# Differential attention: copies of turned probabilities ahead of exponentials, gate and half chunks ending ahead of scores

## The chip, the cores and the metric

One core of a Trainium2 chip runs the whole program. The metric is device time in microseconds (us), the median of several runs. TensorE does the matrix products, VectorE (DVE in the profile) and ScalarE (ACT) the elementwise work, GpSimd (POOL) prepares the weights, SyncE (SP) issues the weight transfers. Each engine works through its own queue in order and waits on semaphores for the others.

## The reference

One step of a streaming encoder with two layers over 544 tokens (512 of a prompt, 32 of a sample), width 1024. The change lies in the second ("odd") layer, whose mixer is, cut down:

```
z = h @ w_in                                    # h: normed input
cq, ck, cv, cg, cr, dq, dk, dv = split(z)       # cg: gate of the linear attention
og = rms_norm(gla(cq, ck, cv, cr)) * silu(cg)   # 4 chunks of 128 features
p  = softmax(mask(q @ k.T / 8))                 # differential attention: 4 heads, 2 maps each
a  = p[:, :, 0] - lam * p[:, :, 1]
od = rms_norm(a @ v) * (1 - lambda_init)
y  = concat([og, od]) @ w_out
x  = x + y
```

The mask is causal by chunks of 64, so the query block b of 128 tokens reads (b + 1) * 128 keys; the sample block reads 128 cached and 32 own keys.

## The kernel before

Activations lie transposed, 128 features on the partitions and 544 tokens along a row. A weight slab is 1024 x 128 numbers, as eight 128 x 128 blocks side by side. Every product with a weight is made of three float32r products (high with high, high with low, low with high), in two halves of 272 tokens: six matmuls (L444, L445, L446), called a **tile** here. GpSimd splits each slab into its high and low part: it waits for `slab_done` of the slab four before (`tick`, L395), writes w_hi in two instructions (L399) and w_lo in two (L404).

The differential attention is a loop of 20 steps u, `OU`: five query blocks b times four heads h. A step needs, in this order: scores S(u) on TensorE (L796, mask L799), the row maxima on VectorE (`odd_max`, L1680, L1682), two exponentials with sums on ScalarE (`odd_exp`, L1169, map 1 before map 0), normalising on VectorE (`odd_normalise`: reciprocal of both sums L1691, map 1 times its factor L1693, difference of the maps L1695), transposes T(u) on TensorE (L858), their copy out of PSUM on ScalarE (`odd_turned`, L1181, L1183, L1184), and the product with the values V(u) on TensorE (L811). Scores, transposes and copy of step u share PSUM banks by u % 2, so S(u + 2) waits for the copy of step u (`pT_out`).

TensorE's queue in step u is T(u), V(u - 1), the fill of place 0, S(u + 2), the fill of place 1, and with h == 1 the sums of squares of the block before (`odd_head_sums`, L818, 0.9 us). A **fill** is weight work with no part in the attention of that step, laid into the loop by the table `ODD_FILL`: ten items in a row, the four chunks of the gate cg (eight tiles each, L444 to L446 on h_both) and then six of the eight chunks m of the output projection's first half (four tiles each, on y_both). The other two, m = 6 and 7, follow the loop. `ODD_FILL[u]` holds the tiles of place 0 and place 1 of step u. All items use accumulator 3 (PSUM banks 6 and 7), so each waits until VectorE has read the one before (`gate_in`, L1719, for a gate chunk, `out_first`, L1280, for an output chunk). A gate chunk and an output chunk with odd m end a slab. With the table of before every item ends at place 1 (item 0 before the loop).

After the gate is read, ScalarE applies silu (`gate_silu`, L1208, with a table load before, and the exp table loaded again after, L916), VectorE multiplies (`gate_mix`, L1723), ScalarE makes the high part (`gate_hi`, L1213) and VectorE the low part (`gate_low`, L1727). Tile c of output chunk 0 waits for the low part of gate chunk c. `head_copy` (L1703), `head_squares` (L1191), `head_rstd` (L1196, L1198), `head_scale` (L1708), `head_hi` (L1203) and `head_low` (L1714) norm the attention's output, once per query block; V of a block's first head waits for `head_copy` of the block before.

VectorE's queue in step u before: `odd_normalise(u + 1)`, `head_copy` (h = 0), `odd_max(u + 2)`, `head_scale` (h = 2), `head_low` (h = 3), `gate_low`, `gate_mix`, and last the reading of an item that ends in step u. ScalarE's queue in step u before: `odd_turned(u)`, `gate_silu`, `gate_hi`, the head parts, and last `odd_exp(u + 2)`. After the loop come m = 6 and 7 (TensorE at 821.54 and 825.70 us of the profile) and the second half of the output projection, `out_chunk` (from 830.01 us).

Of the kernel before, what the change touches and what calls it, by code (L numbers as in the profile page):

```python
# [34 lines left out]
KC = D // P  # L35
# [18 lines left out]
S_EVEN_OUT = EVEN_IN  # L54
# [34 lines left out]
def build(nc, io):  # L89
    ctx = ExitStack()  # L90
    with ctx:
# [146 lines left out]
        def sem(name):  # L238
# [53 lines left out]

        ODD_FILL = {-1: (0, 8), 0: (1, 2), 1: (1, 2), 2: (1, 1), 3: (1, 3), 4: (1, 3), 5: (1, 3), 6: (1, 3),
                    7: (1, 1), 8: (0, 1), 9: (0, 1)} | {u: (1, 1) for u in range(10, 20)}
        FILL_SIZE = [KC] * 4 + [4] * KC
        fill_at, fill_end, done, item = {}, {}, 0, 0
        for u in range(-1, 20):
            for place in range(2):
                count = ODD_FILL[u][place]
                fill_at[u, place] = (item, done, done + count)  # L300
                done += count
                if done == FILL_SIZE[item]:
                    fill_end[u] = item
                    done, item = 0, item + 1
# [130 lines left out]
        def _(pe):  # L435
# [393 lines left out]
            def gla_fill(m, c0, c1):  # L829
                s = S_ODD_OUT + m // 2  # L830
                if c0 == 0:
                    pe.wait_ge(w_ready, s + 1)
                    if m == 0:
                        pe.wait_ge(evac, EVEN_IN + ODD_IN)
                    else:
                        pe.wait_ge(x_upd, X_ODD + m)
                for c in range(c0, c1):
                    if m == 0:
                        pe.wait_ge(gla_lo, c + 1)
                    ins = tiles(3, s, [(4 * (m % 2) + c, y_hi[:, c], y_lo[:, c])], c == 0, c == 3)  # L840
                if c1 == 4:
                    ins.then_inc(slab_done if m % 2 else mid_done, 1)
# [31 lines left out]
            for m in range(KC):  # L874
                pe.wait_ge(x_upd, X_ODD + KC + m - 1)
                out_chunk(S_ODD_OUT + 4 + m // 2, m, 2 + m % 2, d_hi, d_lo, 0)
# [11 lines left out]
        def _(ac):  # L888
# [328 lines left out]
            for u, (b, h) in enumerate(OU):  # L1217
                odd_turned(u)
                if fill_end.get(u - 1, 4) < 4:
                    gate_silu(fill_end[u - 1])  # L1220
                if fill_end.get(u - 2, 4) < 4:
                    gate_hi(fill_end[u - 2])
                if h == 0 and b >= 1:
                    head_squares(b - 1)
                if h == 2 and b >= 1:
                    head_rstd(b - 1)
                if h == 3 and b >= 1:
                    head_hi(b - 1)
                if u + 2 < len(OU):
                    odd_exp(u + 2)  # L1230
            head_squares(4)
# [12 lines left out]
        def _(ve):  # L1244
# [36 lines left out]

            def out_first(s0, m, mid0, upd0):
                if m >= 0:
                    add_out(slab_done if m % 2 else mid_done, (s0 if m % 2 else mid0) + m // 2 + 1, 3, m)

# [256 lines left out]
            for u, (b, c) in enumerate(EU):  # L1542
                if u + 1 < len(EU):
                    even_normalise(u + 1)
                if u in EVEN_FILL:
                    out_first(S_EVEN_OUT, EVEN_FILL[u], 0, 0)
                if c == 0 and b >= 1:
# [3 lines left out]
            for m in range(len(EVEN_FILL), KC):  # L1551
                out_first(S_EVEN_OUT, m, 0, 0)
            even_low(4)
# [130 lines left out]
            def odd_normalise(u):  # L1684

                b, h = OU[u]
                (_, nq), (_, nk), _ = odd_block(b)
                sm = small[0:nq, u % 2]
                p0, p1 = d_probs[u % 2][0:nq, 0, 0:nk], d_probs[u % 2][0:nq, 1, 0:nk]
                ve.wait_ge(e_ready, 20 + 2 * u + 2)  # L1690
                o(ve.reciprocal(sm[:, 20:22], sm[:, 8:10]))  # L1691
                o.wait()
                o(ve.tensor_scalar(p1, p1, sm[:, 21:22], lam[0:nq, 5:6], ALU.mult, ALU.mult))  # L1693
                o.wait()
                o(ve.scalar_tensor_tensor(p0, p0, sm[:, 20:21], p1, ALU.mult, ALU.subtract), p_norm)  # L1695
# [29 lines left out]
            def gate_low(e):  # L1725
                ve.wait_ge(gla_hi, e + 1)
                o(ve.tensor_tensor(y_lo[:, e], o_og[:, e], y_hi[:, e].bitcast(F32), ALU.subtract), gla_lo)  # L1727

            odd_max(0)
            odd_max(1)  # L1730
            odd_normalise(0)
            gate_in(0)
            for u, (b, h) in enumerate(OU):
                if u + 1 < len(OU):
                    odd_normalise(u + 1)
# [6 lines left out]
                if h == 3 and b >= 1:  # L1742
                    head_low(b - 1)
                if fill_end.get(u - 2, 4) < 4:
                    gate_low(fill_end[u - 2])
                if fill_end.get(u - 1, 4) < 4:
                    gate_mix(fill_end[u - 1])
                if u in fill_end:
                    if fill_end[u] < 4:
                        gate_in(fill_end[u])  # L1750
                    else:
                        out_first(S_ODD_OUT, fill_end[u] - 4, KC, 0)
            head_copy(4)
            out_first(S_ODD_OUT, 6, KC, 0)
            head_scale(4)
            out_first(S_ODD_OUT, 7, KC, 0)
            head_low(4)
            ve.wait_ge(head_sum, 10)
            o(ve.memset(sumsq[:, :], 0.0))
# [147 lines left out]
```

## Time and profile before

| what | value |
|---|---|
| median of 3 runs | 1264.03 us (1263.65 to 1266.64) |
| profiled execution, whole | 1263.87 us |
| its span, first to last instruction | 1262.1 us |
| TensorE busy | 1212.3 us, 96% |
| VectorE, ScalarE, GpSimd busy | 749.9, 297.5, 791.3 us |
| granted TensorE clock, mean | 0.991 |

The span leaves out 1.77 us of the whole time. The profile's times count from the first instruction. The loop of the differential attention lies between 728.4 us (first scores) and 821 us, the two items behind it before 830 us.

### The profile page before, as it was taken

How to read it: one execution, taken by the hardware profiler on the slowest of the kernel's cores; microseconds unless marked ns; L12 is line 12 of the kernel's file. 1: busy time of each engine (PE TensorE's matmuls, PEld its weight loads, DVE VectorE, ACT ScalarE, POOL GpSimd, SP SyncE). 2: the span in 40 equal slices, each digit the busy share in tenths (PEclk: the TensorE clock that was granted, in tenths of full speed). 3: DMA queues.
4: the chain of work that ended last, by engine and by line, in shares of the span. 5: the costliest groups of instructions: out<-in, count | busy, mean ns of one | idle time of the engine just before them, and what ended most of it. 6: DMA issues, size and time to landing. Idle time of an engine off the chain costs nothing.

```text
span 1262.1 us, 23492 instructions
## 1 busy us (share of the span) xinstructions
PE 1212.3 (96%) x8605; PEld 1147.3 (91%) x8605; DVE 749.9 (59%) x1299; ACT 297.5 (24%) x628; POOL 791.3 (63%) x932
## 2 busy tenths in 40 slices
PE   6979899999999999999999998999999999999996
PEld 6977799999999999999999986799999999999996
DVE  6987577777777722226524577757778777751112
ACT  3014333222222200002101156423222222210001
POOL 6842258677677667777754442267677767767771
PEclk9989999999999999999999999999999999999999
DMA  6320122322222222333222221132322223223321
GB/s 214 112 65 19 35 84 84 97 86 83 85 97 84 83 95 90 99 100 113 93 92 67 87 68 35 34 111 84 87 94 86 83 86 97 83 85 100 100 83 71
DMA packets 35556, 108.92 MB, mean 86 GB/s; under 512 B 5984, under 2 KB 7824, under 8 KB 35504
## 3 DMA queue, kind: packets, MB, share of 16 engines
q1 hardware_dynamic: 29232, 102.51, 25.8%
q10 hardware_dynamic: 6272, 5.67, 1.5%
q8 instruction: 38, 0.62, 0.2%
q14 instruction: 14, 0.11, 0.0%
HBM read 103.04 MB, written 5.13 MB: 86 GB/s over the span
## 4 chain that ended last, share of the span: by engine, by line
PE 88%; DVE 7%; ACT 2%; issue 1%; DMA 0%; POOL 0%; ACTq 0%; POOLq 0%; DVEq 0%; SPq 0%
PE psum L457 18%; PE psum L455 12%; PE psum L456 12%; PE psum L458 11%; PE psum L459 9%; PE psum L444 7%; PE psum L446 7%; PE psum L445 7%; PE psum L796 1%; DVE even_winsum L1459 1%; DVE probs L1530 1%; PE psum L663 1%; DVE small L1680 0%; DVE x L1280 0%; PE psum L811 0%
## 5 line engine op out<-in xcount | busy, mean ns | idle before, releaser
L404 POOL TENSOR_TENSOR w_lo<-w_raw,w_hi 128x512 fp32r<-128x512 f32 (+1 forms) x370 | 516.3, 1416 | 15.6
L395 POOL TENSOR_TENSOR tick<-tick 1x1 f32<-1x1 f32 x183 | 44.1, 241 | 419.7 <-PE psum L446 212.8
L457 PE MATMUL psum<-h_both,w_hi 128*128 128x480 f32 x704 | 266.8, 379 | 0.0
L399 POOL TENSOR_SCALAR w_hi<-w_raw 128x512 fp32r<-128x512 f32 (+1 forms) x370 | 232.2, 640 | 9.6 <-DMA w_raw<-in_weights 8.2
L455 PE MATMUL psum<-h_both,w_hi 128*128 128x304 f32 x704 | 215.8, 307 | 0.0
L456 PE MATMUL psum<-h_both,w_hi 128*128 128x304 f32 x704 | 212.8, 302 | 0.0
L458 PE MATMUL psum<-h_both,w_lo 128*128 128x304 f32 x704 | 210.9, 300 | 0.0
L444 PE MATMUL psum<-h_both,w_hi 128*128 128x272 f32 x608 | 180.6, 297 | 15.6 <-DVE h_both L1264 10.7
L459 PE MATMUL psum<-h_both,w_lo 128*128 128x240 f32 x704 | 191.5, 272 | 0.0
L446 PE MATMUL psum<-h_both,w_lo 128*128 128x272 f32 x608 | 176.6, 290 | 0.0
L445 PE MATMUL psum<-h_both,w_hi 128*128 128x272 f32 x608 | 175.7, 289 | 0.0
L459 PEld LDWEIGHTS psum<-h_both,w_lo 128*128 128x128 f32 x704 | 131.7, 187 | 20.7
L444 PEld LDWEIGHTS psum<-h_both,w_hi 128*128 128x128 f32 x608 | 115.2, 189 | 20.5 <-issue 17.6
L456 PEld LDWEIGHTS psum<-h_both,w_hi 128*128 128x128 f32 x704 | 133.7, 190 | 0.1
L457 PE MATMUL psum<-y_both,w_hi 128*128 128x480 f32 x352 | 133.4, 379 | 0.0
L455 PEld LDWEIGHTS psum<-h_both,w_hi 128*128 128x128 f32 x704 | 132.3, 188 | 0.1
L457 PEld LDWEIGHTS psum<-h_both,w_hi 128*128 128x128 f32 x704 | 132.3, 188 | 0.0
L458 PEld LDWEIGHTS psum<-h_both,w_lo 128*128 128x128 f32 x704 | 131.8, 187 | 0.0
L1388 DVE TENSOR_TENSOR x<-x,psum 128x240 f32 (+1 forms) x15 | 6.0, 401 | 192.4 <-PE psum L459 192.4
L445 PEld LDWEIGHTS psum<-h_both,w_hi 128*128 128x128 f32 x608 | 115.4, 190 | 0.1
L446 PEld LDWEIGHTS psum<-h_both,w_lo 128*128 128x128 f32 x608 | 115.1, 189 | 0.0
L455 PE MATMUL psum<-y_both,w_hi 128*128 128x304 f32 x352 | 107.7, 306 | 0.0
(245 smaller groups left out, 2268.8 us busy)
## 6 DMA issues: line engine op xcount, KB each, us to landing
w_raw<-in_weights SPq DMA_DIRECT2D x187, 512.0 KB, 3.5
x<-in_x SPq DMA_DIRECT2D x8, 272.0 KB, 5.6
out_y<-x SPq DMA_DIRECT2D x8, 272.0 KB, 2.4
out_diff_v_new<-odd_dv ACTq DMA_DIRECT2D x1, 1024.0 KB, 4.9
out_diff_k_new<-odd_kT ACTq DMA_DIRECT2D x1, 1024.0 KB, 4.7
even_rope<-in_rope ACTq DMA_DIRECT2D x1, 544.0 KB, 3.9
odd_rope<-in_rope ACTq DMA_DIRECT2D x1, 544.0 KB, 4.0
consts<-in_consts ACTq DMA_DIRECT2D x1, 384.5 KB, 5.0
```

The source lines that it names most:

```text
L395: pool.tensor_tensor(tick[:, :], tick[:, :], tick[:, :], ALU.mult).then_inc(ticks, 1)
L399: ins = pool.tensor_scalar(w_hi[:, k, part], w_raw[:, k % RAW, part], 1.0, 0.0, ALU.mult, ALU.add)
L404: ins = pool.tensor_tensor(w_lo[:, k, part], w_raw[:, k % RAW, part], w_hi[:, k, part].bitcast(F32), ALU.subtract)
L444: pe.matmul(out, wh, xh[:, cols], start=first and n == 0, stop=False)
L445: pe.matmul(out, wh, xl[:, cols], start=False, stop=False)
L446: ins = pe.matmul(out, wl, xh[:, cols], start=False, stop=last and n == len(pairs) - 1)
L455: pe.matmul(one, wh, both[:, 0, 0:ONE], start=first, stop=False)
L456: pe.matmul(one, wh, both[:, 1, 0:ONE], start=False, stop=False)
L457: pe.matmul(two, wh, both[:, :, ONE:T], start=first, stop=False)
L458: pe.matmul(one, wl, both[:, 0, 0:ONE], start=False, stop=last)
L459: return pe.matmul(two[:, 0], wl, both[:, 0, ONE:T], start=False, stop=last)
L663: ins = pe.transpose(psum[0:kn, 2 * (u % 2) + kb, j * nq:(j + 1) * nq], pr[0:nq, j, kb * P:kb * P + kn], ident[0:nq, 0:nq])
```

## The change

TensorE: the first fill has seven tiles in place of eight, and step 19 has one more at place 1, so that nine of the ten items end at place 0 (in steps 0, 3, 5, 7, 10, 12, 14, 16, 18) and the tenth at place 1 of step 19. Output chunk 6 goes to accumulator 0 (banks 0 and 1) and waits for no reading. Chunk 7 waits for the reading of chunk 5. The first chunk of the second half doesn't wait for the reading of chunk 7.

ScalarE: `odd_exp(u + 1)` stands behind `odd_turned(u)` in step u, where before `odd_exp(u + 1)` stood at the end of step u - 1, ahead of `odd_turned(u)`. `gate_silu` follows it, and `gate_hi` of an item that ended in step u - 1 is last in step u.

VectorE: an item that ends at place 0 is read first in the step. `odd_normalise` waits for the exponential of map 1, takes its reciprocal and scales, then waits for that of map 0, takes its reciprocal and subtracts: three instructions become four, with a reciprocal of one column for each map in place of one of two, and one more wait. After the loop `head_low(4)` stands ahead of the reading of chunk 7. `gate_mix` and `gate_low` stay at the end of the step.

```
-        ODD_FILL = {-1: (0, 8), 0: (1, 2), 1: (1, 2), 2: (1, 1), 3: (1, 3), 4: (1, 3), 5: (1, 3), 6: (1, 3),
-                    7: (1, 1), 8: (0, 1), 9: (0, 1)} | {u: (1, 1) for u in range(10, 20)}
+        ODD_FILL = {-1: (0, 7), 0: (1, 2), 1: (1, 2), 2: (1, 1), 3: (1, 3), 4: (1, 3), 5: (1, 3), 6: (1, 3),
+                    7: (1, 1), 8: (0, 1), 9: (0, 1), 19: (1, 2)} | {u: (1, 1) for u in range(10, 19)}
...
-                    fill_end[u] = item
+                    fill_end[u, place] = item
...
-                    else:
-                        pe.wait_ge(x_upd, X_ODD + m)
+                    elif m != KC - 2:
+                        pe.wait_ge(x_upd, X_ODD + min(m, KC - 2))
...
-                    ins = tiles(3, s, [(4 * (m % 2) + c, y_hi[:, c], y_lo[:, c])], c == 0, c == 3)
+                    ins = tiles(0 if m == KC - 2 else 3, s, [(4 * (m % 2) + c, y_hi[:, c], y_lo[:, c])], c == 0, c == 3)
...
-                pe.wait_ge(x_upd, X_ODD + KC + m - 1)
+                if m:
+                    pe.wait_ge(x_upd, X_ODD + KC + m - 1)
...
                 odd_turned(u)
-                if fill_end.get(u - 1, 4) < 4:
-                    gate_silu(fill_end[u - 1])
-                if fill_end.get(u - 2, 4) < 4:
-                    gate_hi(fill_end[u - 2])
+                if 1 <= u < len(OU) - 1:
+                    odd_exp(u + 1)
+                if fill_end.get((u, 0), 4) < 4:
+                    gate_silu(fill_end[u, 0])
...
-                if u + 2 < len(OU):
-                    odd_exp(u + 2)
+                if fill_end.get((u - 1, 0), 4) < 4:
+                    gate_hi(fill_end[u - 1, 0])
...
-                ve.wait_ge(e_ready, 20 + 2 * u + 2)
-                o(ve.reciprocal(sm[:, 20:22], sm[:, 8:10]))
+                ve.wait_ge(e_ready, 20 + 2 * u + 1)
+                o(ve.reciprocal(sm[:, 21:22], sm[:, 9:10]))
                 o.wait()
                 o(ve.tensor_scalar(p1, p1, sm[:, 21:22], lam[0:nq, 5:6], ALU.mult, ALU.mult))
+                ve.wait_ge(e_ready, 20 + 2 * u + 2)
+                o(ve.reciprocal(sm[:, 20:21], sm[:, 8:9]))
                 o.wait()
                 o(ve.scalar_tensor_tensor(p0, p0, sm[:, 20:21], p1, ALU.mult, ALU.subtract), p_norm)
...
+            def fill_out(item):
+                if item < 4:
+                    gate_in(item)
+                else:
+                    out_first(S_ODD_OUT, item - 4, KC)
+
             odd_max(0)
             odd_max(1)
             odd_normalise(0)
-            gate_in(0)
             for u, (b, h) in enumerate(OU):
+                if (u, 0) in fill_end:
+                    fill_out(fill_end[u, 0])
                 if u + 1 < len(OU):
                     odd_normalise(u + 1)
...
-                if u in fill_end:
-                    if fill_end[u] < 4:
-                        gate_in(fill_end[u])
-                    else:
-                        out_first(S_ODD_OUT, fill_end[u] - 4, KC, 0)
+                if fill_end.get((u - 2, 0), 4) < 4:
+                    gate_low(fill_end[u - 2, 0])
+                if fill_end.get((u - 1, 0), 4) < 4:
+                    gate_mix(fill_end[u - 1, 0])
+                if (u, 1) in fill_end:
+                    fill_out(fill_end[u, 1])
             head_copy(4)
             out_first(S_ODD_OUT, 6, KC, 0)
             head_scale(4)
-            out_first(S_ODD_OUT, 7, KC, 0)
             head_low(4)
+            out_first(S_ODD_OUT, 7, KC)
```

## Rows read from the trace of the kernel before

**Rows 1.** The page: the chain that ended last, shares by engine.

```profile
PE 88%; DVE 7%; ACT 2%; issue 1%; DMA 0%; POOL 0%; ACTq 0%; POOLq 0%; DVEq 0%; SPq 0%
```

**Rows 2.** Windows: length, each engine's busy time, clock, DMA share, GB/s.

```profile
728.40:830.00 101.60, 89.79 (x656) 74.87 (x654) 74.07 (x141) 54.45 (x142) 33.52 (x43) 1.00 0.16 50
```

**Rows 3.** Timeline of TensorE: start, duration, [idle before <-releaser].

```profile
773.08 0.92 PE L796 MATMUL psum<-odd_kT,d_qT 64*128 64x384 f32 x4 [1.66 <-ACT diff_probsT L1181]
...
777.54 0.92 PE L796 MATMUL psum<-odd_kT,d_qT 64*128 64x384 f32 x4 [1.56 <-ACT diff_probsT L1181]
...
789.01 0.83 PE L811 MATMUL psum<-diff_probsT,odd_dv 128*128 128x128 f32 x6
791.57 0.36 PE L444 MATMUL psum<-y_both,w_hi 128*128 128x272 f32 x1 [1.73 <-DVE x L1280]
...
825.70 0.36 PE L444 MATMUL psum<-y_both,w_hi 128*128 128x272 f32 x1 [0.68 <-DVE x L1280]
...
830.01 0.39 PE L444 MATMUL psum<-diff_hi,w_hi 128*128 128x272 f32 x1 [1.04 <-DVE diff_lo L1714]
```

**Rows 4.** Timeline of TensorE, steps 13 and 14, block 3.

```profile
792.49 1.13 PE L796 MATMUL psum<-odd_kT,d_qT 64*128 64x512 f32 x4
...
793.58 0.39 PE L444 MATMUL psum<-y_both,w_hi 128*128 128x272 f32 x1
...
794.45 0.60 PE L858 MATMUL psum<-consts,diff_probs 128*128 128x128 f32 x4
794.88 1.06 PE L811 MATMUL psum<-diff_probsT,odd_dv 128*128 128x128 f32 x8
795.69 0.37 PE L444 MATMUL psum<-y_both,w_hi 128*128 128x272 f32 x1
```

**Rows 5.** Timeline of GpSimd around the end of gate chunk 0.

```profile
736.77 0.18 POOL L395 TENSOR_TENSOR tick<-tick 1x1 f32<-1x1 f32 x1 [4.17 <-PE psum L446]
736.93 1.19 POOL L399 TENSOR_SCALAR w_hi<-w_raw 128x512 fp32r<-128x512 f32 x2
738.20 2.58 POOL L404 TENSOR_TENSOR w_lo<-w_raw,w_hi 128x512 fp32r<-128x512 f32 x2
```

**Rows 6.** Timeline of VectorE: an undisturbed normalising, then that stretch.

```profile
734.36 0.35 DVE L1693 TENSOR_SCALAR diff_probs<-diff_probs,small,lam 128x128 f32<-128x128 f32 x1
734.74 0.35 DVE L1695 SCALAR_TENSOR_TENSOR diff_probs<-diff_probs,small 128x128 f32<-128x128 f32 x1
736.64 0.72 DVE L1719 TENSOR_TENSOR gate_raw<-psum,rstd 128x544 f32<-128x544 f32 x1 [1.55 <-PE psum L446]
...
737.47 0.73 DVE L1693 TENSOR_SCALAR diff_probs<-diff_probs,small,lam 128x128 f32<-128x128 f32 x1
738.24 1.40 DVE L1695 SCALAR_TENSOR_TENSOR diff_probs<-diff_probs,small 128x128 f32<-128x128 f32 x1
```

**Rows 7.** Timeline of VectorE, block 3: normalising and maxima.

```profile
797.40 0.17 DVE L1691 RECIPROCAL small<-small 128x2 f32<-128x2 f32 x1 [1.57 <-ACT diff_probs L1169]
797.61 0.55 DVE L1693 TENSOR_SCALAR diff_probs<-diff_probs,small,lam 128x512 f32<-128x512 f32 x1
798.19 0.75 DVE L1695 SCALAR_TENSOR_TENSOR diff_probs<-diff_probs,small 128x512 f32<-128x512 f32 x1
799.15 1.23 DVE L1680 TENSOR_REDUCE small<-psum 128x2 f32<-128x1024 f32 x1 [0.21 <-PE psum L799]
```

**Rows 8.** Timeline of ScalarE: table load, silu, load, head_hi, exponential.

```profile
767.61 1.28 ACT L1208 ACT_TABLE_LOAD   x1
768.91 0.66 ACT L1208 ACTIVATE gate_raw<-gate_raw 128x544 f32<-128x544 f32 x1
769.58 1.28 ACT L916 ACT_TABLE_LOAD   x1
770.87 0.63 ACT L1203 ACTIVATE diff_hi<-head_tmp 128x512 fp32r<-128x512 f32 x1
771.41 0.58 ACT L1169 ACTIVATE diff_probs<-psum,small 128x384 f32<-128x384 f32 x1
```

More of the change, by code:

```diff
@@ L1280, in add_out, with out_first @@
                 ve.tensor_tensor(halves(x[:, m]), halves(x[:, m]), pair(acc), ALU.add).then_inc(x_upd, 1)
-            def out_first(s0, m, mid0, upd0):
-                if m >= 0:
-                    add_out(slab_done if m % 2 else mid_done, (s0 if m % 2 else mid0) + m // 2 + 1, 3, m)
+            def out_first(s0, m, mid0, acc=3):
+                add_out(slab_done if m % 2 else mid_done, (s0 if m % 2 else mid0) + m // 2 + 1, acc, m)
             def out_norm(s0, mid0, n, early):
@@ L1545, in _ @@
                 if u in EVEN_FILL:
-                    out_first(S_EVEN_OUT, EVEN_FILL[u], 0, 0)
+                    out_first(S_EVEN_OUT, EVEN_FILL[u], 0)
                 if c == 0 and b >= 1:
@@ L1551, in _ @@
             for m in range(len(EVEN_FILL), KC):
-                out_first(S_EVEN_OUT, m, 0, 0)
+                out_first(S_EVEN_OUT, m, 0)
             even_low(4)
@@ L1743, in _ @@
                     head_low(b - 1)
[L1744 to L1747, printed above, removed]
-                if u in fill_end:
-                    if fill_end[u] < 4:
-                        gate_in(fill_end[u])
-                    else:
-                        out_first(S_ODD_OUT, fill_end[u] - 4, KC, 0)
+                if fill_end.get((u - 2, 0), 4) < 4:
[4 more added lines that the diff above has]
+                    fill_out(fill_end[u, 1])
             head_copy(4)
```

## The prediction

> **What bounds the kernel now.** I read the chain that ended last first: TensorE holds 88% of it [rows 1], so time is won only where TensorE waits. Then the windows over the loop and the items behind it [rows 2]: 101.6 us, TensorE busy 89.8, clock 1.00 throughout, so that 11.8 us of waiting is all that this stage can give (0.9% of the span), and the clock gives nothing. VectorE is busy 74.1 us, ScalarE 54.5: neither is full, the waits are matters of order. Then TensorE's timeline, for who ended each wait: 15 stalls, of which 5 are shown [rows 3]; the first (0.44 us, ahead of the scores of step 1) is not touched. The reader is to see two kinds: scores held by the copy of the turned probabilities (773.08, 777.54), and a fill held by VectorE's reading of accumulator 3 (791.57, 825.70), and last 830.01. A stall costs more than its idle column, since that counts from the modelled end of a matmul and the next could have started before: the six matmuls at 789.01 need about 0.6 us (three quarters of the 0.81 of eight, 794.88 to 795.69 [rows 4]), so the fill should start at 789.6 and starts at 791.57: 1.97 lost, 1.73 idle [rows 3]. Counted so, the 14 stalls in reach cost 13.75 us.
>
> **Unit costs.** TensorE, start to start in block 3 [rows 4]: scores 1.09, a tile 0.87, transposes 0.43, values 0.81, a tile behind values about 0.93. Other blocks go by the same differences in the same timeline. VectorE in block 3 [rows 7]: reciprocal 0.21, scaling 0.58, difference 0.75, maxima 1.26 and 0.17 behind them. An item read by VectorE costs 0.72, 0.64 until its next instruction starts [rows 6]. ScalarE: the table load, silu and table load of a gate take from 767.61 to 770.87, 3.26 us [rows 8].
>
> **What each part takes away.** (a) The copy ahead of the exponential: the copy of step u needs T(u) alone and no longer waits for the maxima of u + 1. That ends the kind at 773.08 and 777.54. Six stalls of this kind cost 8.2 us (1.91, 1.81, 1.29, 0.84, 0.35 and the 1.97 at 791.57, where VectorE's reading stood behind the same chain). (b) Items ending at place 0: the reading runs under the scores behind it (0.46 to 1.1 us), not in the open. Four stalls behind gates cost 2.7. (c) Behind the loop, accumulator 0 for chunk 6, chunk 7 released by chunk 5, the second half released early: 0.40, 0.80 and 1.2 go, 2.4 in all; head_low(4) now ends about 1 us before TensorE needs it, so nothing replaces them. The two stalls left are 0.5.
>
> **What it puts in their place.** I went through the loop step by step with these costs, each engine in its new order. What TensorE loses anew:
>
> (1) Weights against normalising. When a slab ends, GpSimd's tick starts 0.46 us behind the start of its last matmul, w_hi takes 1.19, and the first half of w_lo starts 1.9 behind it [rows 5]. In that stretch VectorE's scaling took 0.73 instead of 0.35 and its difference 1.40 instead of 0.35 [rows 6]: it ended 1.44 after w_lo had begun. So an item read first and a normalising behind it end 3.35 us behind the slab's last matmul in block 0, 3.6 in blocks 2 and 3. Before, the normalising hit was that of u + 2, needed one full step later. Now it is that of u + 1, and TensorE has only the rest of the tile, S(u + 2) and place 1 until T(u + 1). With three tiles at place 1 that covers (steps 3, 5). With one it doesn't. Step 7: slab's last matmul 767.05, p_norm 770.64, TensorE ready 769.12: T(8) loses 1.65. Step 12: 790.91, 794.65, ready 793.10: T(13) loses 1.68. Step 16: 809.91, 813.25, ready 811.98: T(17) loses 1.4. Step 0, two tiles: T(1) loses 0.65. Sum 5.4. The bounds of such a meeting are no delay at all (0.35, [rows 6]) and both halves of w_lo (2.58, [rows 5], 1.3 more at each place); I take one half, as in the row, since the difference comes at the same point of the split as there.
>
> The new reciprocal (0.21) delays the difference by less than its split wins, but the difference is then issued about 2.1 behind that matmul, still later than 1.9. The Trainium skill, "SBUF — State Buffer", section "Who interferes with whom", speaks against this change: a VectorE instruction with two SBUF inputs and a GpSimd one that reads SBUF exclude each other for a whole instruction, and whichever came first holds the ports. The trace agrees. The same rule would let VectorE win if it came 0.2 us sooner; that is the second rival.
>
> (2) ScalarE's order. `gate_hi` now stands last in ScalarE's step and waits for `gate_mix`, last in VectorE's step, behind the maxima of S(u + 2). The next copy stands behind it. In steps 1, 4 and 6, with more fill, that costs 0.41, 0.31 and 0. In step 8 it has no cover: the silu of chunk 3 holds ScalarE until 771.25, head_hi follows, so the copy of step 8 ends at 772.29 and S(10) loses 0.96; the exponential of 9 follows, and T(9) loses 0.63. VectorE then ends its difference at 774.67, head_copy, maxima and gate_mix at 777.0, gate_hi at 777.6, the copy of 9 at 778.09, while TensorE could have started S(11) at 775.7: 2.5 lost. Sum 4.8. The page "ScalarE: Activation LUTs", section "What ACT_TABLE_LOAD costs", puts about 2.7 us on each switch, against 1.28 here [rows 8]; by it the S(10) loss would be some 2.8 larger, but the silu starts 0.02 behind the load in this trace, and I go by the trace.
>
> (3) Readings that are not covered. The scores of steps 14, 16 (32 queries) last 0.4 us, and step 18 has none: readings at places 14, 16 and 18 cost 0.58, 0.58 and 1.05, and the normalising behind them, now second in VectorE's queue, T(15) 0.76, T(19) 0.23, and the head_copy behind it V(16) 0.4. At 0 and 3, 0.53 and 0.32. Sum 4.45.
>
> (4) Small ones: T(4) 0.12, a reading in step 7 0.10, gate_low of chunk 3 ahead of the tile in step 10 0.16, T(11) 0.44, T(12) 0.11, V(12) 0.17. Sum 1.1.
>
> New losses 5.4 + 4.8 + 4.45 + 1.1 = 15.75 us against 13.75: 2.0 us more. The work itself is the same: 56 tiles in the loop, moved only. The second half should begin at 831.9 instead of 830.01. Behind that nothing changes. On GpSimd's and SyncE's queues nothing is added or passed: each slab's split and the load behind it move with the end of the slab four before, and a split takes 4.0 us (736.77 to 740.78 [rows 5]); the latest, released by chunk 5 at 824.6 and by chunk 7 at 831.8, are wanted by the fourth and sixth chunk of the second half, over 9 us later. The profiled execution would take 1263.87 + 2.0 = 1265.9, the median 1264.03 + 2.0 = 1266.0. The 23 small differences may each be wrong by 0.1 to 0.2 us, and a few by more, since one late link moves the next: 1263 to 1269 for this case.
>
> **Rivals.** About 0.3%, 3.8 us, is what a measurement of this kernel tells from no change.
>
> First, it works as built, chance 0.15. The new order removes the 8.2 + 2.4 and most of the 2.7, and the new stalls are half of mine (VectorE slack of 27 us in the stage speaks for it: 101.6 - 74.1 [rows 2]; against it stand the orders of (1) and (2)): 13.75 - 7.9 = 5.9 gained, 1258; with next to none, 1253.
>
> Second, the collision of (1) alone is missed, chance 0.12: the difference needs to be issued 0.2 us earlier than I place it, or w_lo later. Then T(8), T(13), T(17) lose about 1 us less each and T(1) 0.4: 3.4 less, 1262.6. Against it, VectorE lost both times in [rows 6], the scaling too. With a 2 us shorter wait at S(11) as well it would pass into the first.
>
> Third, slower, chance 0.20: VectorE's step takes longer than its sum where gate_mix ends it. Margins are small: in step 6 the wait of S(9) for gate_hi is hidden by 0.2 us, in steps 1, 4 and 8 it is already bare, and each 0.1 us that VectorE is later is paid at four places. From 0.45 us per step on the change is slower by more than 3.8 (2.0 + 4 x 0.45); at 1 us it gives 1270. For it speaks that gate_mix has two SBUF inputs and may meet GpSimd; against it, that GpSimd is done by then, 4.6 us behind the slab.
>
> Fourth, the stage's ends are hidden by something later, so that neither gain nor loss is seen, 1264, chance 0.03. Little speaks for it, with TensorE at 88% of the chain.
>
> **Numbers.** My case has 0.50, nearly all within 0.3%. Faster by over 0.3%: the first, 0.15. Slower: the third and the tail of mine, 0.23. Within: 0.62. The likeliest time is 1266.0. With a tenth left out on either side the range goes from 1257 (into the first rival) to 1270.5 (the third at its full price).
>
> **What would show it.** Right: no wait of scores for the copy except in steps 8 and 9 with some 2.5 us ahead of S(11); transposes that wait 1.4 to 1.7 us for VectorE at T(8), T(13) and T(17), with differences of 1.4 us or more beside w_lo; no stall between the last values and the second half, which is 7.2 us behind them instead of 9.5. Wrong: T(8), T(13), T(17) on time, or the second half beginning before 829 us.

## The result, and the profile after

The changed kernel takes 1268.43 us (median of 21 runs, 1264.63 to 1272.47), the kernel before 1264.64 (21 runs, 1263.62 to 1271.0): ratio 1.0032, interval 1.0023 to 1.0042, so 4.0 us slower (3.8 by the two medians; all differences below that are given beside a ratio come from the ratio). The forecast was 1266.0, with 1257 to 1270.5 as its range, and "within 0.3%" with a chance of 0.62; it came out inside the range and just past 0.3%, on the side to which I had given 0.23.

Of the changed kernel's page, the span, the granted clock in 40 slices, and the chain that ended last [rows 1]:

```profile
span 1269.3 us, 23511 instructions
...
PEclk9989899999999999999999999899999999999999
...
PE 87%; DVE 8%; ACT 2%; issue 1%; DMA 1%; POOL 0%; ACTq 0%; POOLq 0%; DVEq 0%; SPq 0%
```

The profiled execution took 1271.06 us, more than the median: its losses are of the right kind, but more of them than in a typical run. The clock row shows what the stage lacked before: the 26th slice (793 to 825 us) reads 8. (The fifth slice, 127 to 159 us, reads 8 too, where the kernel before reads 9: clock falls also occur in the first 150 us, in both kernels and differently from run to run, so the mean clock of a whole run is only a rough sign of what happened in this stage.) The windows over the stage, with the columns of [rows 2], say where:

```profile
765.00:790.00 25.00, 21.43 (x139) 16.12 (x138) 19.76 (x39) 15.85 (x36) 4.15 (x5) 0.93 0.07 22
790.00:813.00 23.00, 19.00 (x135) 14.46 (x133) 17.21 (x38) 10.22 (x30) 7.07 (x10) 1.00 0.08 23
813.00:820.00 7.00, 6.46 (x24) 4.60 (x24) 2.80 (x10) 1.52 (x7) 1.19 (x1) 0.53 0.27 77
820.00:826.00 6.00, 5.09 (x26) 3.84 (x25) 2.48 (x7) 2.98 (x11) 0.00 (x0) 0.78 0.00 0
826.00:832.00 6.00, 6.00 (x31) 5.92 (x31) 1.37 (x3) 0.31 (x1) 1.42 (x4) 0.63 0.00 0
```

The third number from the end of each row, the granted clock, is 0.93, 1.00, 0.53, 0.78 and 0.63, where before the whole stage had 1.00 [rows 2]. The row of 813 to 820 us holds 24 matmuls in 6.46 busy us. In TensorE's timeline they are seen one by one: 128x272 matmuls of 0.29 us that start every 0.13 us become 0.43 us every 0.23 us, the lower of the two levels, 1.2 GHz:

```profile
813.12 0.27 PE L858 MATMUL psum<-consts,diff_probs 32*128 32x32 f32 x2 [1.13 <-DVE diff_probs L1697]
813.81 0.60 PE L811 MATMUL psum<-diff_probsT,odd_vc 128*128 128x32 f32 x2 [0.42 <-DVE head_tmp L1705]
814.34 0.63 PE L811 MATMUL psum<-diff_probsT,odd_dv 32*128 32x32 f32 x2
814.90 0.59 PE L444 MATMUL psum<-y_both,w_hi 128*128 128x272 f32 x1
815.30 0.43 PE L445 MATMUL psum<-y_both,w_hi 128*128 128x272 f32 x1
815.52 0.43 PE L446 MATMUL psum<-y_both,w_lo 128*128 128x272 f32 x1
```

In windows of 0.5 us the clock falls three times: from 772.5 to 775.6 us, in the wait ahead of S(10); from 813.4 to 820.2, straight behind the wait of 1.13 us for the transposes of step 17 (first row) and in the 0.42 for head_copy (second row); and from 823.7 to 830.5, behind a wait of 0.91 for the reading at place 1 of step 18. Not every long wait has a fall behind it: S(11) (1.25) and T(13) (1.49) have none. The other long waits of the changed kernel, with the columns of [rows 3]:

```profile
770.73 0.55 PE L858 MATMUL psum<-consts,diff_probs 128*128 128x128 f32 x3 [1.39 <-DVE diff_probs L1697]
...
772.56 1.66 PE L796 MATMUL psum<-odd_kT,d_qT 64*128 64x384 f32 x4 [0.84 <-ACT diff_probsT L1182]
...
778.22 0.92 PE L796 MATMUL psum<-odd_kT,d_qT 64*128 64x384 f32 x4 [1.25 <-ACT diff_probsT L1182]
```

```profile
794.53 0.66 PE L858 MATMUL psum<-consts,diff_probs 128*128 128x128 f32 x4 [1.49 <-DVE diff_probs L1697]
...
802.99 0.36 PE L444 MATMUL psum<-y_both,w_hi 128*128 128x272 f32 x1 [0.51 <-DVE x L1281]
...
804.42 0.65 PE L858 MATMUL psum<-consts,diff_probs 128*128 128x128 f32 x4 [0.45 <-DVE diff_probs L1697]
```

The two waits of [rows 3] for the copy (1.66, 1.56) have become 0.84 and 1.25 in the same two steps, and a new kind stands beside them, transposes that wait for L1697, the difference of the maps. 770.73 is T(8), 772.56 S(10), 778.22 S(11), 794.53 T(13), 813.12 T(17). (S(10), 1.66 us long where the same scores took 0.92 in [rows 3], already ran at the lower clock.) At the end there is no wait: the last values start at 830.21, the second half at 837.29, 7.1 us, where it was 9.5.

The collision that T(8), T(13) and T(17) wait for, GpSimd and VectorE in the changed kernel, in the form of [rows 5, 6]:

```profile
767.56 0.18 POOL L395 TENSOR_TENSOR tick<-tick 1x1 f32<-1x1 f32 x1 [6.32 <-PE psum L446]
767.71 1.20 POOL L399 TENSOR_SCALAR w_hi<-w_raw 128x512 fp32r<-128x512 f32 x2
768.99 2.81 POOL L404 TENSOR_TENSOR w_lo<-w_raw,w_hi 128x512 fp32r<-128x512 f32 x2
```

```profile
767.51 0.72 DVE L1721 TENSOR_TENSOR gate_raw<-psum,rstd 128x544 f32<-128x544 f32 x1 [1.38 <-PE psum L446]
768.15 0.15 DVE L1691 RECIPROCAL small<-small 128x1 f32<-128x1 f32 x1
768.34 0.78 DVE L1693 TENSOR_SCALAR diff_probs<-diff_probs,small,lam 128x384 f32<-128x384 f32 x1
769.04 0.14 DVE L1695 RECIPROCAL small<-small 128x1 f32<-128x1 f32 x1
769.22 1.45 DVE L1697 SCALAR_TENSOR_TENSOR diff_probs<-diff_probs,small 128x384 f32<-128x384 f32 x1
```

VectorE reads the gate first (0.72), the scaling takes 0.78 instead of 0.48, and the difference, issued 0.23 us behind w_lo, 1.45 instead of 0.62. The two undisturbed times are those of the next step of the kernel before:

```profile
772.97 0.48 DVE L1693 TENSOR_SCALAR diff_probs<-diff_probs,small,lam 128x384 f32<-128x384 f32 x1
773.49 0.62 DVE L1695 SCALAR_TENSOR_TENSOR diff_probs<-diff_probs,small 128x384 f32<-128x384 f32 x1
```

### The profile page after: what moved, and what is told of

Its sections match the earlier page's. It is cut to its first block, busy times and chain, and to the rows that moved or that the text cites. A ratio compares the mean times of both kernels' runs of the same rounds, so it can differ in the third digit from the quotient of the medians.

```text
span 1269.3 us, 23511 instructions
## 1 busy us (share of the span) xinstructions
PE 1221.0 (96%) x8605; PEld 1154.2 (91%) x8605; DVE 749.8 (59%) x1319; ACT 297.2 (23%) x628; POOL 791.3 (62%) x932
## 4 chain that ended last, share of the span: by engine, by line
PE 87%; DVE 8%; ACT 2%; issue 1%; DMA 1%; POOL 0%; ACTq 0%; POOLq 0%; DVEq 0%; SPq 0%
PE psum L457 18%; PE psum L455 12%; PE psum L456 12%; PE psum L458 11%; PE psum L459 9%; PE psum L444 7%; PE psum L446 7%; PE psum L445 7%; PE psum L811 1%; DVE probs L1530 1%; DVE even_winsum L1459 1%; PE psum L796 1%; PE psum L663 1%; DVE diff_probs L1697 1%; DVE x L1281 0%
```

## The experiments

Twelve kernels ran, all beside the kernel before. "Stage" below is the time from the first scores of the loop to the first product of the second half in the profile of each: 101.1 us before (728.87 to 830.01; the first scores start at 728.87, and 728.4, as given further up, is only where the windows begin), 107.9 in the changed kernel's profiled run (729.42 to 837.29). "Loop" is its part from the first scores to the last values: 91.6 us before.

**1. The end alone.** The kernel before with the new part behind the loop:

```
-                    else:
-                        pe.wait_ge(x_upd, X_ODD + m)
+                    elif m != KC - 2:
+                        pe.wait_ge(x_upd, X_ODD + min(m, KC - 2))
...
-                    ins = tiles(3, s, [(4 * (m % 2) + c, y_hi[:, c], y_lo[:, c])], c == 0, c == 3)
+                    ins = tiles(0 if m == KC - 2 else 3, s, [(4 * (m % 2) + c, y_hi[:, c], y_lo[:, c])], c == 0, c == 3)
...
-                pe.wait_ge(x_upd, X_ODD + KC + m - 1)
+                if m:
+                    pe.wait_ge(x_upd, X_ODD + KC + m - 1)
...
-            out_first(S_ODD_OUT, 6, KC, 0)
+            add_out(mid_done, KC + 4, 0, 6)
             head_scale(4)
+            head_low(4)
             out_first(S_ODD_OUT, 7, KC, 0)
-            head_low(4)
```

> The kernel before with only the part behind the loop changed: chunk 6 to accumulator 0, chunk 7 released by chunk 5, the second half not waiting for chunk 7, head_low(4) ahead of the reading of chunk 7. My reading: the three stalls there (0.40, 0.80, 1.2 us) go and nothing replaces them, 2.4 us less than before, about 1262.2, ratio 0.998; the second half starts 7.2 us behind the last values instead of 9.5. Rival (the end is hidden by something later): 1264.6, ratio 1.000.

Measured: 1261.04, ratio 0.998 (0.9971 to 0.9989), 2.5 us faster. Stage 98.8 us. None of the three waits is left. (Its profile has a fall of the clock as well, 0.83 from 790 to 800 us, behind the old wait for the reading of chunk 1, still 1.73 us; its loop, 91.9 us, is only 0.3 longer for it.) The part is worth what was forecast, and the changed kernel contains it: all else in it costs more than the net shows.

**2. The copy ahead of the exponential alone.**

```
                 odd_turned(u)
+                if 1 <= u < len(OU) - 1:
+                    odd_exp(u + 1)
...
-                if u + 2 < len(OU):
-                    odd_exp(u + 2)
```

> The kernel before with one edit: in ScalarE's queue the copy of step u stands ahead of the exponential of u + 1. Table of fills, readings and normalising as before. My reading: of the 8.2 us of stalls where scores waited for the copy, those in blocks 2 and 3 mostly go (1.81, 1.29, 0.84 and a part of 1.97); the one in step 8 stays near 1 us, since the silu of chunk 3 still stands between: 4 to 6 us less than before, 1259 to 1261, ratio 0.996. Rival (VectorE is the bound, so the wait turns up at the transposes instead): within 1 us of before.

Measured: 1263.96, ratio 0.9999 (0.999 to 1.0008). My reading fell, the rival's was right. TensorE's waits in this kernel, in blocks 2 and 3:

```profile
772.48 0.55 PE L858 MATMUL psum<-consts,diff_probs 128*128 128x128 f32 x3 [0.83 <-DVE diff_probs L1695]
...
773.87 0.92 PE L796 MATMUL psum<-odd_kT,d_qT 64*128 64x384 f32 x4 [0.39 <-ACT diff_probsT L1181]
...
776.36 0.55 PE L858 MATMUL psum<-consts,diff_probs 128*128 128x128 f32 x3 [0.59 <-DVE diff_probs L1695]
...
782.52 0.36 PE L444 MATMUL psum<-y_both,w_hi 128*128 128x272 f32 x1 [0.57 <-DVE x L1280]
```

```profile
792.25 0.37 PE L444 MATMUL psum<-y_both,w_hi 128*128 128x272 f32 x1 [1.54 <-DVE x L1280]
...
802.06 0.36 PE L444 MATMUL psum<-y_both,w_hi 128*128 128x272 f32 x1 [0.29 <-DVE x L1280]
```

The scores hardly wait for the copy any more (0.39 in place of 1.66), but the transposes now wait for VectorE (0.83, 0.59) and the fills for its reading (0.57, 1.54, 0.29). The stall went from ScalarE's link of the ring to VectorE's. The loop takes 91.3 us, 0.3 less than before, at a clock of 1.00.

**3. gate_hi one step later in the changed kernel.**

```
-                if fill_end.get((u - 1, 0), 4) < 4:
-                    gate_hi(fill_end[u - 1, 0])
...
+                if fill_end.get((u - 2, 0), 4) < 4:
+                    gate_hi(fill_end[u - 2, 0])
                 if fill_end.get((u, 0), 4) < 4:
```

> The changed kernel with gate_hi one step later, behind the exponential, so that the copy of the next step no longer waits for gate_mix. My reading: the 2.2 us wait of S(11) falls to about 0.5 and the small ones in steps 2 and 5 go, 2 to 2.5 us less than the changed kernel, about 1266, ratio 1.001. Rival (S(11) is held by head_copy and head_squares or by VectorE in any case): no difference to the changed kernel, ratio 1.003.

Measured: 1265.63, ratio 1.0021 (1.001 to 1.0032), some 1.4 us less than the changed kernel (2.8 by the medians). S(11) no longer appears among TensorE's waits, so the cause is as read; T(8), T(13) and T(17) still wait (1.39, 1.48, 1.12), and the clock is 0.63 from 813 to 820. With intervals of 1.4 us either way the size is only roughly known, and a part of it may be the clock: seven of its ten runs have a mean clock of 0.987 or 0.988, against ten of the changed kernel's 21.

**4 and 5. TensorE kept busy in its waits.** Both leave the order and the waits of the changed kernel alone and add matmuls whose output nobody reads, nine at the end of step 16 in the first, and in the second:

```
+            def keep_busy(n, bank):
+                for _ in range(n):
+                    pe.matmul(psum[:, bank, 0:HALF], h_hi[:, 0, 0:P], h_hi[:, 0, 0:HALF], start=True, stop=True)
...
                 odd_fill(u, 0)
+                keep_busy({8: 6, 9: 14}.get(u, 0), 5)
+                keep_busy({18: 6}.get(u, 0), 1)
...
                     odd_head_sums(b - 1)
+                keep_busy({7: 10, 12: 10, 16: 9}.get(u, 0), 5)
```

> The changed kernel with nine matmuls of 272 columns more at the end of step 16, into bank 5 that nobody reads then, where TensorE waited 1.3 us for the transposes of step 17: no work on the path, only less idle time. Theory that the fall of the granted clock (0.53 from 813 to 820 us, 0.63 from 826 to 832) comes from the idle time in steps 16 to 18: the clock stays 1.00 there, runs near 1271 vanish, median 1265 to 1266.5, ratio 1.001. Rival (the clock falls for other reasons, or the idle in steps 18 and 19 does it): median and spread as the changed kernel, 1268.4, ratio 1.003, clock below 1 behind 820 us at least.

> The changed kernel with matmuls of 272 columns laid into all its long waits of TensorE, into banks that nobody reads then: 10 at the end of step 7, 6 and 14 ahead of the scores of steps 8 and 9, 10 at the end of step 12, 9 at the end of step 16, 6 ahead of place 1 of step 18. The order of the real work and its waits stay. Theory (the stalls cost about 1 to 2 us by themselves, and the rest of the measured 4 us is the granted clock that falls after them): the clock is 1.00 from 765 to 838 us, all runs lie between 1264.3 and 1266.5, median 1265.0, ratio 1.001. Rival (falls of the clock are not tied to this idle time): runs of 1268 and more remain as in the kernel with nine matmuls in step 16 alone.

Measured: with the nine 1265.57, ratio 1.0014 (1.0002 to 1.0026), none of 11 runs above 1268.43 where nine of the changed kernel's 21 lie above 1270. In its profile the clock is 1.00 from 790 to 838 and 0.84 from 779 to 790, behind the wait of S(11) that had no filling. That wait is 1.76 us there, at a clock of 1.00 all the way to it. With all 55: 1264.85, ratio 1.0002 (0.9994 to 1.0011), ten of 11 runs between 1263.6 and 1265.3, all of these with a mean clock of 0.991. Of the 24 runs of the kernel before that were taken beside it only eight have that; the others have 0.986 to 0.990. Its windows:

```profile
765.00:779.00 14.00, 13.22 (x96) 10.54 (x94) 10.39 (x22) 10.21 (x22) 4.18 (x5) 1.00 0.13 38
779.00:790.00 11.00, 10.91 (x75) 8.28 (x74) 9.36 (x20) 6.02 (x15) 0.00 (x0) 1.00 0.01 2
790.00:813.00 23.00, 21.23 (x152) 16.57 (x150) 17.25 (x36) 9.85 (x29) 7.53 (x10) 1.00 0.08 24
813.00:820.00 7.00, 6.44 (x41) 4.91 (x41) 3.23 (x12) 3.73 (x15) 0.78 (x1) 1.00 0.24 75
820.00:826.00 6.00, 6.00 (x44) 5.63 (x45) 3.01 (x7) 1.20 (x4) 1.53 (x4) 1.00 0.01 3
826.00:832.00 6.00, 6.00 (x50) 6.00 (x50) 2.07 (x4) 0.99 (x3) 3.00 (x4) 1.00 0.37 108
```

The clock stays at 1.00 throughout. Stage 102.2 us, 1.0 more than before. So 55 useless matmuls made the kernel 0.3% faster: 1.0032 to 1.0002, 3.8 us (with an interval of some 1.6 us either way).

They move none of the real work. Counted from the first scores, S(11) starts at 48.80 us in the changed kernel's profile and at 48.83 in this one, T(17) at 83.70 and 83.77. So the changed kernel's first fall (772.5 to 775.6) cost nothing, since the wait of S(11) behind it is shorter by as much (1.25 instead of 1.76), and the 5.7 us between the two stages (107.9 and 102.2) arise wholly behind T(17), where the clock is low for 13.6 us. At a clock of 1.00 the changed order makes the loop 3.6 us longer (95.2 against 91.6) and the new end makes the rest 2.6 us shorter (6.95 against 9.54).

**6 and 9. GpSimd in pieces of 256 columns,** on the changed kernel and on the kernel before:

```
-PIECE = 512
+PIECE = 256
```

> The changed kernel with GpSimd splitting a slab in pieces of 256 instead of 512 columns: four instructions for w_hi and four for w_lo. Theory (VectorE's difference waits for one whole w_lo instruction, about 1.3 us, because both read SBUF through a shared way that one instruction holds): the difference beside a w_lo takes some 0.9 to 1.0 us instead of 1.45 to 1.57, and T(8), T(13), T(17) wait about 0.6 us less each, 1.5 us less in all. Rival (the slowdown is a sharing of bandwidth): the difference stays at 1.4 us or more and the waits stay. More instructions on GpSimd may cost something elsewhere, so the waits in the trace decide, not the time.

> The kernel before with GpSimd splitting in pieces of 256, nothing else: is the 3 us that this edit won on the changed kernel a matter of the changed order? Theory (it shortens a collision that only the new order has on the path): within 1 us of before, 1263.5 to 1264.5, ratio 1.000, since in the kernel before the delayed normalising had a full step in hand. Rival (a general gain or loss of the finer split): 2 us or more to either side.

Measured: on the changed kernel 1264.49, ratio 0.9996 (0.9988 to 1.0005), 4.5 us less than without; on the kernel before 1263.84, ratio 0.9995 (0.9986 to 1.0004), no difference. In the changed one, GpSimd, VectorE and TensorE around T(8):

```profile
767.07 0.18 POOL L395 TENSOR_TENSOR tick<-tick 1x1 f32<-1x1 f32 x1 [5.19 <-PE psum L446]
767.22 1.61 POOL L399 TENSOR_SCALAR w_hi<-w_raw 128x256 fp32r<-128x256 f32 x4
768.91 3.01 POOL L404 TENSOR_TENSOR w_lo<-w_raw,w_hi 128x256 fp32r<-128x256 f32 x4
```

```profile
768.67 0.62 DVE L1697 SCALAR_TENSOR_TENSOR diff_probs<-diff_probs,small 128x384 f32<-128x384 f32 x1
```

```profile
769.34 0.55 PE L858 MATMUL psum<-consts,diff_probs 128*128 128x128 f32 x3 [0.50 <-DVE diff_probs L1697]
```

The difference takes 0.62, as if alone, and GpSimd's w_hi is longer: 1.61 for four pieces, against 1.19 for the two. Most of that is no meeting with VectorE, since four pieces take 1.50 elsewhere in this profile (at 705.4, 824.0 and 831.0): four instructions cost more than two. So w_lo begins 1.84 us behind the tick instead of 1.43, and the difference, issued 1.60 behind it (1.66 before), comes first. That is what the second rival asked for, by a w_lo that is later. The theory for this run, a shorter wait for a shorter instruction, was hardly tested by it: the meeting didn't take place. T(8) waits 0.50 instead of 1.39, T(13) 0.61 instead of 1.49, T(17) not at all. That is more than expected, and it is not a sharing of bandwidth: where the difference overlaps the start of w_lo it keeps its full speed (0.62, and 0.75 at T(13)), and w_lo takes 3.01 and 3.16 instead of 2.82. What T(8) won was in good part lost again at the next link: S(10) now waits 1.73 us for the copy, which stands behind the silu of chunk 3, where it waited 0.84. And the 4.5 us are not those waits alone: in this profile the clock falls behind S(11) (0.89 from 779 to 790 us) but stays at 1.00 behind step 17, where the changed kernel's fell twice. The two parts are not separated.

**7. The reading behind the normalising in the changed kernel.**

```
-                if (u, 0) in fill_end:
-                    fill_out(fill_end[u, 0])
                 if u + 1 < len(OU):
                     odd_normalise(u + 1)
+                if (u, 0) in fill_end:
+                    fill_out(fill_end[u, 0])
```

> The changed kernel with VectorE's normalising of u + 1 ahead of the reading of an item that ended at place 0, in place of behind it. My reading: T(8), T(13), T(17) no longer wait (1.65, 1.68, 1.4), but the fill of place 1 behind the scores waits for the reading, 1.0 to 2 us in steps 3, 5, 7, 12, 14, 16, 18: the same or 1 to 3 us slower than the changed kernel, ratio 1.004. Rival (the reading first was the error): 3 to 4 us faster than the changed kernel, ratio 1.000.

Measured: 1269.72, ratio 1.0044 (1.003 to 1.0058). As expected, the transposes no longer wait, the fills do, with 1.85, 1.85, 1.79, 1.36 and 1.70 us ahead of place 1 of steps 3, 5, 7, 12 and 14 (0.51 and 0.91 in steps 16 and 18, as in the changed kernel). So the place of the reading is not the error; an item that ends ahead of the scores leaves VectorE two jobs for the same short stretch, and one of them is late.

**8 and 10. What of the change pays.** The kernel before with the new end, the copy ahead and the normalising in halves, and the old table of fills; in number 8 the reading stands straight behind the maxima too, in number 10 where it was. The edit that number 8 has and number 10 has not:

```
                     odd_max(u + 2)
+                if u in fill_end:
+                    if fill_end[u] < 4:
+                        gate_in(fill_end[u])
+                    else:
+                        out_first(S_ODD_OUT, fill_end[u] - 4, KC, 0)
```

> The kernel before with the new part behind the loop, the copy ahead of the exponential, the normalising in two halves, and the reading of an item (which ends at place 1, as before) moved from the end of VectorE's step to straight behind the maxima. Table of fills, gate_silu, gate_hi and gate_mix as before. Expected: 2.8 us from the end, and since the reading no longer stands behind head_scale, head_low, gate_low and gate_mix, the 1.5 us ahead of chunk 2 and the 0.5 us ahead of others shrink: 1259 to 1260.5, ratio 0.9965, faster than both kernels. Rival (the copy ahead buys nothing in any form): as the end alone, 1261.0, ratio 0.998.

> The mixed kernel of before (new end, copy ahead, normalising in halves) with the reading left at the end of VectorE's step as in the kernel before: what is the moved reading worth? Theory (the reading's place is what lets the copy ahead pay): 1260.5 to 1261.2, ratio 0.998, that is 1 to 1.5 us more than the mixed kernel. Rival (the normalising in halves did it): 1259.6, ratio 0.9966.

Measured: number 8 1259.65, ratio 0.9966 (0.9954 to 0.9978); number 10 1258.74, ratio 0.9958 (0.9945 to 0.9972). The moved reading is worth nothing that can be told apart, and number 10's theory fell: the normalising in halves is what lets the copy ahead pay, as its rival had it. At a clock of 1.00 in all three profiles, the loop of number 10 takes 89.3 us, against 91.6 before and 91.3 with the copy ahead alone. In number 8 the wait for the reading of chunk 1 is 0.62 and T(8) waits 1.73, in number 10 they are 1.73 and 0.91:

```profile
771.77 0.55 PE L858 MATMUL psum<-consts,diff_probs 128*128 128x128 f32 x3 [1.73 <-DVE diff_probs L1698]
...
789.61 0.36 PE L444 MATMUL psum<-y_both,w_hi 128*128 128x272 f32 x1 [0.62 <-DVE x L1281]
...
793.23 0.66 PE L858 MATMUL psum<-consts,diff_probs 128*128 128x128 f32 x4 [0.59 <-DVE diff_probs L1698]
```

```profile
771.01 0.55 PE L858 MATMUL psum<-consts,diff_probs 128*128 128x128 f32 x3 [0.91 <-DVE diff_probs L1698]
...
772.52 0.92 PE L796 MATMUL psum<-odd_kT,d_qT 64*128 64x384 f32 x4 [0.52 <-ACT diff_probsT L1182]
...
774.82 0.55 PE L858 MATMUL psum<-consts,diff_probs 128*128 128x128 f32 x3 [0.40 <-DVE diff_probs L1698]
...
790.14 0.36 PE L444 MATMUL psum<-y_both,w_hi 128*128 128x272 f32 x1 [1.73 <-DVE x L1281]
```

**12. The normalising in halves alone** on the kernel before:

```
-                ve.wait_ge(e_ready, 20 + 2 * u + 2)
-                o(ve.reciprocal(sm[:, 20:22], sm[:, 8:10]))
+                ve.wait_ge(e_ready, 20 + 2 * u + 1)
+                o(ve.reciprocal(sm[:, 21:22], sm[:, 9:10]))
...
+                ve.wait_ge(e_ready, 20 + 2 * u + 2)
+                o(ve.reciprocal(sm[:, 20:21], sm[:, 8:9]))
```

> The kernel before with only the normalising in two halves (it starts at the exponential of map 1; two reciprocals of one column). The order alone won nothing and end, order and halves together won 5.8 us, end alone 2.8. Theory (halves and order work only together: with the old order the scores still wait for the copy, which the halves don't touch): within 1 us of before, ratio 0.9995. Rival (the halves are worth their 2.5 to 3 us alone): 1261.5, ratio 0.998.

Measured: 1266.15, ratio 1.0014 (1.0005 to 1.0023). Slower, which neither had. Its waits are those of the kernel before, entry by entry:

```profile
773.64 0.92 PE L796 MATMUL psum<-odd_kT,d_qT 64*128 64x384 f32 x4 [1.65 <-ACT diff_probsT L1181]
...
778.18 0.92 PE L796 MATMUL psum<-odd_kT,d_qT 64*128 64x384 f32 x4 [1.64 <-ACT diff_probsT L1181]
```

but the clock is 0.84 from 779 to 790 in its profile, behind the second of these waits, and only one of its 11 runs has the mean clock of 0.991. Up to that point nothing is lost: S(11) starts 48.7 us behind the first scores in both kernels; the stage then takes 102.8 us against 101.1. So in this profile the loss is the clock's, and the halves by themselves neither win nor lose. The same waits had a fall of the clock behind them in the profile of number 1, and none in those of the kernel before and number 9; of the 15 runs of the kernel before that stand beside this one, seven have 0.991. Why it falls in more runs here isn't shown.

**11. The best of these.** Number 8 with pieces of 256:

> The mixed kernel (new end, copy ahead, normalising in halves, reading straight behind the maxima, old table) with pieces of 256: its waits of 1.73 us at T(8) and 0.59 at T(13), both behind a difference of 1.4 to 1.6 us beside w_lo, shrink by 1 and 0.6: 1258 to 1259, ratio 0.9955. Rival (more instructions on GpSimd cost elsewhere): 1259.7 or more.

Measured: 1258.38, ratio 0.9949 (0.9936 to 0.9963), 6.4 us faster than before and 10 us faster than the changed kernel. T(8) waits 0.34, T(13) not at all, and S(10), which didn't wait in number 8, 1.08. The time is as expected, but it isn't told apart from that of number 8 or of number 10.

## Why the prediction was right, and where it was off

**The end** (2.4 us): right, 2.5 measured alone, and 7.1 us between the last values and the second half against 7.2 forecast.

**Weights against normalising:** right in place, mechanism and size. With the 0.55 us by which the whole stage began later taken off, T(8) came at 770.2 (forecast 770.8), T(13) at 794.0 (794.8), T(17) at 812.6 (813.4); the difference ended 1.44 to 1.87 behind the start of w_lo, against 1.44 to 1.84 taken in the forecast. (Its "3.6 in blocks 2 and 3" is 3.74 for step 12 in its own times, 790.91 to 794.65; 3.76 was measured.) The finer split shortened those waits or removed them, and helped only the kernel that has them on its path. The margin that the second rival stood on, 0.2 us, was 0.23 at T(8) (769.22 against 768.99), and the finer split turned it round.

**ScalarE's order:** right in kind. S(10) began at 772.0 (772.4) and S(11) at 777.7 (778.2). With gate_hi moved the wait of S(11) is gone. Its size was taken too long: 2.5 us lost in the forecast, 1.76 idle where the clock was 1.00 up to it (number 4), or about 2.0 lost with the 0.24 that the forecast counts above the idle column at 791.57.

**Uncovered readings:** as forecast, 0.51, 0.51 and 0.91 idle at places 14, 16 and 18, 0.45 at T(15).

**What the change takes away, (a):** the gross sum of 8.2 us was right as a list of waits that vanish, and it was set against new ones, so the net didn't suffer. But as a worth it would have been wrong: the copy ahead alone removed most of these waits and won nothing, the halves alone lost 1.8 us (by the clock, in the profile), and both on top of the end brought 2.8 us (0.998 to 0.9958), which the loop times at a clock of 1.00 bear out (0.3 us for the copy ahead, 2.3 for both). The two edits act on one ring, scores, maxima, exponential, normalising, transposes, copy, scores; loosening one link lets the next hold.

**The net by order alone** was forecast as 2.0; the stage with the clock held up is 1.0 us longer than before, and the median 0.3 to 0.6 us above before, which isn't told apart from no change. It was mis-sized by some 1 us: the times above are 0.4 to 0.8 us earlier than forecast, and T(8) was already 0.6 early, so most of the error lies in the waits up to there.

**The step that failed** is the second sentence of the prediction: "clock 1.00 throughout, [...] and the clock gives nothing". It read a level of one profile of the kernel before as a property of the stage, and the sum has no term for the clock. The change put waits of TensorE behind each other in steps 8 and 9 (1.39, 0.84 and 1.25 us idle) and 17 and 18 (1.13, 0.42, 0.91), and the clock fell within both groups. The experiment with all waits filled puts 3.8 us on it (1.0032 against 1.0002), nearly the whole of the 4.0 measured. So that the measured time lies inside the range, and that the kernel is slower at all beyond the noise, is luck as far as the sum goes: its own 2.0 us were 1.0 or less. The third rival ended near the measured time, but by another cause: VectorE's step was not longer than its sum (S(11) came 0.5 us earlier than forecast, not later), and it deserves no credit.

What stays open: what decides from run to run whether the clock falls (the same changed kernel gives 1264.6 and 1272.5 us, and its ten runs with the same mean clock of 0.988 still lie between 1264.6 and 1268.4), and why it falls in more runs with the halves alone.

## What to carry to other kernels

Where TensorE is the bound and the other engines feed it in a ring, count a wait removed as won only when the next link has slack; two edits that win nothing alone can win together, so try them in pairs before dropping either. Work that another engine must do between two fixed points belongs at the point from which the longest stretch of covered TensorE work follows, and an item's end fixes three such jobs at once: its reading, the release of its weights, and the port use of whoever prepares the next. And price idle time of TensorE twice, once as waiting and once as the clock that may fall behind it: a few matmuls into a free bank show in one experiment how much of a slowdown is the second, if the real work ahead of the fall keeps its times, as it did here.

## What the runs showed of the hardware

The granted clock fell to 1.2 GHz within or behind waits of 0.8 to 1.8 us that follow another wait by a few us (0.84 ahead of S(10), 1.13 ahead of T(17), 0.91 in step 18; 1.76 ahead of S(11) in number 4, 1.64 in number 12), in a stage in which TensorE is otherwise busy, and it stayed there for 3.1, 6.8 and 6.8 us (772.5, 813.4 and 823.7 in the changed kernel's profile; 128x272 matmuls started every 0.23 us instead of 0.13), although TensorE was busy from soon after the fall to the rise. It did so in some runs and not in others: of the changed kernel's 21 runs, the ten up to 1268.42 us have a mean clock of 0.988, the nine above 1270 us 0.981 to 0.984. Matmuls that compute nothing of use held it up: with 55 of them the profile has 1.00 throughout the stage, and ten of 11 runs a mean of 0.991. A low clock that ends before a wait can be free, as it was ahead of S(11).

A VectorE instruction with both inputs in SBUF that comes 0.2 us behind the start of a GpSimd 128x512 subtraction takes 1.45 us instead of 0.62. With pieces of 128x256 GpSimd's instructions for w_hi take 1.50 us in all instead of 1.19, so the subtraction began later, the VectorE instruction came before it and took its normal 0.62. The Trainium skill, "SBUF — State Buffer", section "Who interferes with whom", says that a VectorE instruction with two SBUF inputs contends with a GpSimd one that reads SBUF, for a port pair which is locked exclusively, and that whoever issues first holds it for the whole instruction while the other is blocked. These runs agree: the difference at 769.22 ended 1.68 us behind the start of the subtraction, of which two take 2.81, so 0.27 behind the first of them. Who comes first is then a matter of tenths of a microsecond, and a thing to tune. The finer split cost the kernel before nothing (0.9995) and gave the changed one 4.5 us, of which an unknown part is the clock; what a shorter GpSimd instruction is worth where the two do meet was not measured.
